# A two-block transformer kernel: two norms of the latent stream merged, and the matrix memory's unit loop reordered

## What is computed

```python
def rms_norm(x, gain=None):
    y = xf * lax.rsqrt(jnp.mean(xf * xf, axis=-1, keepdims=True) + EPS)
    ...
    y = y * gain
# end of block 1, start of block 2 (layer 0)
x = rms_norm(x, final_gain)
u_lat = rmsnorm(h_lat, norms[layer]) * (1 + scale_l[:, None]) + shift_l[:, None]
u_ctx = rmsnorm(h_ctx, norms[layer]) * (1 + scale_c) + shift_c
```

```python
w_intra = jnp.exp(logw - m_t[..., None])
qk = jnp.einsum('bhtd,bhsd->bhts', qc, kc) * w_intra
num = jnp.einsum('bhts,bhsv->bhtv', qk, vc) + ...
h = num / jnp.maximum(jnp.abs(den), jnp.exp(-m_t))[..., None]
```

## Time and profile before

| | us |
|---|---|
| median of 3 runs | 2748.92 (2747.24 to 2751.9) |
| the profiled execution, own time | 2751.43 |
| its span in the profile | 2749.6 |
| PE busy, share of the span | 91% |
| DVE busy | 60% |
| ACT busy | 37% |
| mean granted clock of PE | 0.969 |

### The profile page before, as it was taken

How to read it: one execution, slowest core, us unless ns; L and a number is a source line. 1 busy time by engine, 2 the same in 40 slices (tenths; PEclk the granted TensorE clock), 3 DMA queues, 4 the chain that set the end, 5 groups by cost and what they waited for, 6 DMA issues and landing times.

```text
span 2749.6 us, 49023 instructions
## 1 busy us (share of the span) xinstructions
PE 2509.0 (91%) x19510; PEld 2053.9 (75%) x19510; DVE 1650.3 (60%) x2694; ACT 1010.2 (37%) x1630; POOL 380.0 (14%) x336
## 2 busy tenths in 40 slices
PE   6999999978888799999899999889999998889976
PEld 4888877747777588888788887669987865667856
DVE  3777766465554577778677743665543335445665
ACT  4222223353342442222422223455444244334344
POOL 2000010114451200001100001020013500020041
PEclk8999999989999999999999999999999999989999
DMA  7666662200000256666466643225561320013401
GB/s 264 222 193 193 199 180 81 74 1 4 4 4 3 92 155 195 192 193 204 141 194 192 191 140 92 62 85 166 180 181 57 97 88 23 1 61 119 128 7 47
DMA packets 88429, 323.48 MB, mean 118 GB/s; under 512 B 9712, under 2 KB 10864, under 8 KB 87504
## 3 DMA queue, kind: packets, MB, share of 16 engines
q1 hardware_dynamic: 86864, 310.68, 36.5%
q0 software_dynamic: 1408, 10.59, 1.1%
HBM read 320.17 MB, written 1.05 MB: 117 GB/s over the span
## 4 chain that ended last, share of the span: by engine, by line
PE 82%; DVE 9%; ACT 5%; issue 2%; DMA 1%; DVEq 1%; POOL 0%; ACTq 0%; SPq 0%
PE bank L391 22%; PE bank L392 22%; PE bank L393 22%; PE bank L1770 3%; PE bank L1052 1%; PE bank L1043 1%; DVE row_statistics L1093 1%; DMA weight_ring<-stream_k 1%; PE bank L1066 1%; ACT work L1154 1%; ACT work L1163 1%; PE bank L1438 1%; PE bank L596 1%; DVE work L2655 1%; ACT weights_hi_lo L343 1%
## 5 line engine op out<-in xcount | busy, mean ns | idle before, releaser
L343 ACT ACTIVATE weights_hi_lo<-weight_ring 128x1024 fp32r<-128x1024 f32 (+1 forms) x388 | 404.0, 1042 | 1189.3 <-PE bank L393 1180.0
L391 PE MATMUL bank<-input_hi,weights_hi_lo 128*128 128x512 f32 (+1 forms) x2080 | 768.4, 369 | 44.6 <-DVE input_lo L622 38.7
L348 DVE TENSOR_TENSOR weights_hi_lo<-weight_ring,weights_hi_lo 128x1024 fp32r<-128x1024 f32 (+1 forms) x372 | 451.6, 1214 | 572.0 <-ACT weights_hi_lo L343 571.2
L392 PE MATMUL bank<-input_lo,weights_hi_lo 128*128 128x512 f32 (+1 forms) x2080 | 764.4, 368 | 0.0
L393 PE MATMUL bank<-input_hi,weights_hi_lo 128*128 128x512 f32 (+1 forms) x2080 | 763.7, 367 | 0.0
L391 PEld LDWEIGHTS bank<-input_hi,weights_hi_lo 128*128 128x128 f32 x2080 | 398.6, 192 | 117.5 <-issue 50.0
L392 PEld LDWEIGHTS bank<-input_lo,weights_hi_lo 128*128 128x128 f32 x2080 | 398.6, 192 | 62.5 <-issue 0.5
L393 PEld LDWEIGHTS bank<-input_hi,weights_hi_lo 128*128 128x128 f32 x2080 | 398.1, 191 | 62.9
L391 PE MATMUL bank<-hidden_hi_lo,weights_hi_lo 128*128 128x512 f32 (+1 forms) x960 | 345.4, 360 | 27.2 <-DVE hidden_hi_lo L832 17.6
L392 PE MATMUL bank<-hidden_hi_lo,weights_hi_lo 128*128 128x512 f32 (+1 forms) x960 | 343.9, 358 | 0.0
L393 PE MATMUL bank<-hidden_hi_lo,weights_hi_lo 128*128 128x512 f32 (+1 forms) x960 | 343.7, 358 | 0.0
(11 more groups left out here) (458 smaller groups left out, 2854.7 us busy)
## 6 DMA issues: line engine op xcount, KB each, us to landing
weight_ring<-stream_k SPq DMA_DIRECT2D x498, 512.0 KB, 3.5
weight_ring<-stream_f SPq DMA_DIRECT2D x64, 448.0 KB, 3.4
weight_ring<-stream_f SPq DMA_DIRECT2D x32, 512.0 KB, 3.7
extra_tiles<-condrows POOLq DMA_DIRECT2D x3, 1024.0 KB, 5.6
constants<-consts POOLq DMA_DIRECT2D x1, 2112.5 KB, 9.4
residual_stream<-xin SPq DMA_DIRECT2D x1, 2048.0 KB, 11.4
work<-nabias POOLq DMA_DIRECT2D x1, 2048.0 KB, 8.7
residual_stream<-ctx POOLq DMA_DIRECT2D x1, 1024.0 KB, 6.8
```

The source lines that it names most:

```text
L343: act.activation(split_place(place)[:, 0, 0:words], w[:, 0:words], ACT.Copy).then_inc(hi_ready, 1)
L348: eng.tensor_tensor(split_place(place)[:, 1, 0:words], ring[:, n % RING, 0:words], split_place(place)[:, 0, 0:words].bitcast(F32), ALU.sub ...
L391: pe.matmul(out, weights[:, 0, w], x_hi, start=first, stop=False)
L392: pe.matmul(out, weights[:, 0, w], x_lo, start=False, stop=False)
```

## The change

**Norms.** The gain norm and `norm 6` become one step, `two_norms_*`. While the feed-forward's last products run, ACT squares each tile twice: all 512 columns as it is, and the latent 256 columns with the gain on them (`gained_square`). POOL adds both kinds. PE sums both. The two roots are then made from one pair of sums: ACT takes the logarithm of the plain sum, DVE multiplies the square of the first root with the gained sum, ACT takes that logarithm, DVE adds the two, and ACT takes one exponential for all columns. The gain is folded into the modulation scale of the latent columns. The gained latent tiles themselves, which the residual stream needs later, are written by DVE after the norm (`gained_tiles_vector`, 8 instructions), ahead of the stage's loop. The second table load and the 8 squares behind the gain norm are gone.

**Matrix memory.** Rows and masked diagonals alternate between two places (`pb[0]` and `pb[5]`, two tiles `RD`), and there are three sets of weights. The scores of a head are made once for both directions (4 matmuls of 512, 512, 256 and 256 columns, in `pb[2]` to `pb[4]`) and no longer per unit. ACT waits for `sums(u-3)` where it waited for `normalise(u-2)`; PE's row waits for the exponentials of two units ago. DVE's loop now masks unit u+1 ahead of weighing unit u.

```diff
-                dve.wait_ge(qk_ready, u + 1)
+                dve.wait_ge(qk_ready, u // 2 + 1)
...
             for u in range(len(UNITS)):
-                weigh(u)
                 if u + 1 < len(UNITS):
                     mask_diagonal(u + 1)
+                weigh(u)
                 if u:
                     normalise(u - 1)
...
-                if u >= 2:
-                    act.wait_ge(unit_done, u - 1)
+                if u >= 3:
+                    act.wait_ge(sums_ready, u - 2)
...
-                if u:
-                    pe.wait_ge(exps_ready, u)
-                pe.matmul(pb[0][:, :], SELROW[:, 4 * d + h, :], RBR, start=True, stop=True).then_inc(rows_spread, 1)
+                if u >= 2:
+                    pe.wait_ge(exps_ready, u - 1)
+                pe.matmul(pb[ROW_BANKS[u % 2]][:, :], SELROW[:, 4 * d + h, :], RBR, start=True, stop=True).then_inc(rows_spread, 1)
...
             scores(0)
+            spread_rows(1)
             for u in range(len(UNITS)):
-                if u + 1 < len(UNITS):
+                if u and u + 1 < len(UNITS):
                     spread_rows(u + 1)
-                    scores(u + 1)
+                if u % 2 and u + 1 < len(UNITS):
+                    scores((u + 1) // 2)
                 sums(u)
```

```diff
+        def two_norms_scalar(act, x0):
...
+            act.wait_ge(summed, 7)
+            act.activation(logs, pb[2][:, :], ACT.Ln, bias=epsb[:, 0:1], scale=1.0 / D)
+            act.drain()
+            act.activation(squares, logs[:, a:b], ACT.Exp, scale=-1.0).then_inc(two_norms, 1)
+            act.activation(FIRST_RMS, logs[:, a:b], ACT.Exp, scale=-0.5)
+            act.wait_ge(two_norms_added, 1)
+            act.activation(squares, squares, ACT.Ln, bias=epsb[:, 0:1], scale=1.0 / D).then_inc(two_norms, 1)
+            act.wait_ge(two_norms_added, 2)
+            act.activation(pb[3][:, :], logs, ACT.Exp, scale=-0.5).then_inc(rooted, 1)
...
+        def two_norms_vector(dve):
...
+            dve.wait_ge(two_norms, 1)
+            dve.tensor_tensor(squares, squares, pb[0][:, 0:TC], ALU.mult).then_inc(two_norms_added, 1)
+            dve.wait_ge(two_norms, 2)
+            dve.tensor_tensor(logs, logs, squares, ALU.add).then_inc(two_norms_added, 1)
...
-            norm_scalar(act, 6, "l0_in", scaled, GAIN_NORMS[0][2] * KT + 1)
+            norm_scalar(act, 6, "l0_in", ffn_added, 4 + 3 * KT + 1)
```

More of the change, by code:

```diff
@@ L555, in norm_scalar @@
                 last_squares(act, cols, x_ready, x0, stage)
-            root(act, cols, bank, place)
+            if n != 6:
+                root(act, cols, bank, place)
             if n == 0:
@@ L574, in norm_scalar @@
                     ins.then_inc(modulated, 1)
-        ADDED_PLACES = [place for place in range(len(NORMS) + len(GAIN_NORMS)) if place != 7]
+        ADDED_PLACES = list(range(len(NORMS) + len(GAIN_NORMS)))
         def add_squares_gpsimd(pool, cols, place):
@@ new lines, in two_norms_tensor @@
+        def two_norms_tensor(pe):
+            pe.wait_ge(squares_added, ADDED_PLACES.index(6) + 1)
+            pe.matmul(pb[0][:, 0:TC], V("ones", 0, P), GAINED_SQ[:, 0, :], start=True, stop=False)
+            pe.wait_ge(gained_squared, KT)
+            pe.matmul(pb[0][:, 0:TC], V("ones", 0, P), GAINED_SQ[:, KT - 1, :], start=False, stop=True)
+            sum_squares(pe, ALL, 2, 6)
+        def two_norms_vector(dve):
+            a, b = LAT
+            logs, squares = WORK[:, 0, a:b], WORK[:, 1, 0:TC]
+            first_splits_vector(dve, "l0_in")
+            dve.wait_ge(two_norms, 1)
+            dve.tensor_tensor(squares, squares, pb[0][:, 0:TC], ALU.mult).then_inc(two_norms_added, 1)
+            dve.wait_ge(two_norms, 2)
+            dve.tensor_tensor(logs, logs, squares, ALU.add).then_inc(two_norms_added, 1)
@@ new lines, in gained_tiles_vector, with two_norms_gpsimd @@
+        def gained_tiles_vector(dve):
+            a, b = LAT
+            dve.drain()
+            for kt in range(KT):
+                dve.scalar_tensor_tensor(out=X[:, kt, a:b], in0=X[:, kt, a:b], scalar=V("fgain", kt), in1=FIRST_RMS,
+                                         op0=ALU.mult, op1=ALU.mult)
+        def two_norms_gpsimd(pool):
+            for kt in range(1, KT - 1):
+                pool.wait_ge(squared, 6 * KT + kt + 1)
+                pool.tensor_tensor(SQ[:, 0, :], SQ[:, 0, :], SQ[:, kt, :], ALU.add)
+                pool.wait_ge(gained_squared, kt + 1)
+                pool.tensor_tensor(GAINED_SQ[:, 0, :], GAINED_SQ[:, 0, :], GAINED_SQ[:, kt, :], ALU.add)
+                pool.drain()
+            pool.drain().then_inc(squares_added, 1)
@@ L1173, in build, with rotate @@
         q_copied, k_copied, v_copied = sem("mla_query_copied"), sem("mla_key_copied"), sem("mla_value_copied")
[L1174 to L1177 removed]
+        ODD_HEADS = 8
+        def rotate(dve, jobs, scale, scratch, turned, before=0):
             for i, (x, bank, cos, sin) in enumerate(jobs):
@@ L1182, in rotate @@
                                          op1=ALU.mult)
-                dve.wait_ge(turned, i + 1)
+                dve.wait_ge(turned, before + i + 1)
                 dve.scalar_tensor_tensor(out=tmp[:, TC:T], in0=bank[:, TC:T], scalar=scale, in1=sin, op0=ALU.mult,
@@ L2220, in mask_diagonal @@
                 dve.wait_ge(rows_spread, u + 1)
-                dve.tensor_tensor(tiles(RD), tiles(pb[0][:, :]), over(C("nu" if UNITS[u][0] == 0 else "nl"), TT), ALU.add)\
+                dve.tensor_tensor(tiles(RD[u % 2]), tiles(pb[ROW_BANKS[u % 2]][:, :]), over(C("nu" if UNITS[u][0] == 0 else "nl"), TT), ALU.add)\
                    .then_inc(rd_ready, 1)
```

105 lines of the change are left out of this document (64 added, 41 removed).

## The result

The changed kernel takes 2765.73 us (median of 5 runs, 2759.32 to 2770.22), beside 2750.94 for the kernel before on the same chip (5 runs, 2747.24 to 2752.16). The ratio is 1.0054, with a 95% interval of 1.0037 to 1.0071: slower by 14.8 us, between 10 and 20. The profiled execution has 2763.22 of its own, a span of 2761.4 and a mean granted clock of 0.965. That is 11.8 above the one before, where the sum said 11.1.

What follows compares the result with a forecast made beforehand. PE was 91% busy with 82% of the chain, but a short chain set the norms and a DVE-ACT circle the matrix memory. Norms -7.3 plus memory +18.4 (circle +6.4, clock +12) gave +11.1: 2760.0 us, range 2754 to 2768.

Steps and rivals of the forecast that it cites:

- Norms, -7.3: At the two norms: DVE's first scaling comes at 2061.26 instead of 2068.55, 7.3 us earlier.
- What this needs stays covered: Around the norms: doubled squares, POOL's doubled adds and DVE's gained tiles stay hidden, cost taken as zero.
- The later edges of the clock may differ by 1 us either way; zero taken: Behind the norms: later clock edges may shift time by 1 us either way, counted as zero.
- 1.6 us more of waiting: Before PE's products behind the norms: PE waits 4.3 us now and 1.6 more after, for four more steps.
- The circle at full clock, +6.4: Matrix memory: a pair takes 16.6 us instead of 12.72; +7.0, start +0.4, last sums -1.0, giving +6.4.
- The waits of 4.3 and 2.6: Matrix memory, each pair: PE waits 4.3 us before the even sums and 2.6 before the scores.
- The clock, +12: Matrix memory: PE's clock falls behind six waits, units 1 to 6, at 2.0 us each, +12.
- +3 and +26: Matrix memory's clock term: low end three falls at 1.0 us, high end six whole bursts at 1.2 GHz.
- The clock holds: Rival, matrix memory: full clock through most of the circle, one or two falls; +1, 2750 us; chance 0.18.
- The rows come in time: Rival, matrix memory: DVE's mask finds its row ready, a pair takes about 10.5 us; 2735 us; chance 0.10.
- The clock stays down: Rival, matrix memory: PE stays at 1.2 GHz for the stage; +25, 2774 us; chance 0.07.
- The norms give nothing back: Rival, norms: PE's products are held as long as before, +11 becomes +18; 2767 us; chance 0.05.

Runs made afterwards that it cites:

- memory only: The kernel before with only the matrix memory's new section, its two norms left as they were: 2772.12 us, ratio 1.0076.
- e8_adds_later: Changed kernel with row u+2 spread ahead of sums u, and POOL's gained adds of tiles 1 to 5 delayed to fall between DVE splits: 2737.64 us.
- e9_rows_old_norms: Kernel before with the new matrix memory, row u+2 spread ahead of sums u, and the old separate norms: 2743.75 us, ratio 0.9973.
- e4_rows_two_ahead: Changed kernel with PE spreading the row of unit u+2 ahead of the sums of unit u: 2734.18 us, ratio 0.9944 to the kernel before.
- e5_filled: Changed kernel with unread products filling PE's waits before even sums and odd scores, and ACT copying turned heads one unit earlier: 2751.63 us.
- e6_filled_long: Changed kernel with unread products filling only PE's long waits, before the sums of even units: 2759.49 us, ratio 1.0020 to the kernel before.
- e1_norms_only: Changed kernel with the old matrix memory, so only the two norms are merged: 2745.37 us, ratio 0.9982 to the kernel before.

## Why the prediction was right, and where it was not

**Norms, -7.3.** Measured -7.5 in their place: 15.29 to 7.78. From the last square to the scaling pass 6.82, for 7.04 in the sum. The step that failed is "What this needs stays covered", at zero. POOL's doubled adds were looked for between ACT and PE, where they cost nothing. They cost 0.9 by running into a split of DVE in the feed-forward before. The gained tiles are hidden: they end at 2075.86, and the next split starts at 2077.50. "The later edges of the clock may differ by 1 us either way; zero taken" came out at 0.5: PE waits 6.27 before its first product, where it waited 4.36, and over the first 5 us of products the granted clock is 0.50 (2062.5 to 2067.5), where it was 0.66 (2071 to 2076). From the first product to the copy of the values pass 280.77 us, for 280.30 before. (The prediction has 1.6 us more of waiting and so 5.9. Its own four added steps and their hand-overs make 1.9, which is what came.) So -7.5 + 0.9 + 0.5 = -6.1. The pairs of kernels that differ in the norms alone give, by their ratios, -4.9, -6.1 (changed, and memory only), -6.6 (`e8_adds_later` and `e9_rows_old_norms`) and -8.0 (`e4_rows_two_ahead` and `e9_rows_old_norms`). By their intervals the first is uncertain by about 2.4 us, the others by about 5, so they bear -6.1 out but can't tell it from -7.5.

**The circle at full clock, +6.4.** Measured +6.7 by `e5_filled`. There sums of odd units start 16.77 apart, for 16.6 in the sum, and from unit 1 to 7 pass 45.28 us (2357.11 to 2402.39), for 44.6. That makes +7.7 against the kernel before for +7.0, the start is +0.7 for +0.4, and the end -1.7 for -1.0. The waits of 4.3 and 2.6 are 4.23 and 2.44. The sum takes only one of the falls of the kernel before out, the last sums; what the longer circle costs with all of them out is the 10 us above.

**The clock, +12.** Measured +12.2 as the difference of two stages. Behind the six waits the bursts lost, against the same shapes at full clock, 2.6, 1.4, 0, 2.2, 1.5 and 2.2 (scores of 5.49, 2.85 and 4.39 for 2.85; sums of 3.87, 4.64 and 4.64 for 2.47). That is 9.9, or 1.65 for each where 2.0 was taken. The rest is one more fall, at the first sums behind a seventh wait of 2.44 (4.09 for 2.50, 1.6), which the sum had not counted, and what the bursts dragged along (a turned head 1.00 for 0.60, sums 2.75 for 2.40). By the section of the Trainium skill that the prediction names (page "TensorE: Matmul & The Clock Gate", section "HAM oscillation — how this bites in real kernels") every burst would start cold. The trace agrees for some and not for others (2.85 behind 2.44 us of waiting, 5.49 behind the same). So the total is hit within 0.2 by luck, by two errors that cancel: each fall too dear, and one fall missed. The ends that the prediction works out for this term, +3 and +26, would give 2751 and 2774; the stated range of 2754 to 2768 is a choice between them. Between two kernels with the same matrix memory, the changed one and the memory alone, the stage is the same to 0.1 (80.17, 80.24), and the same bursts run long (in the memory alone sums 3.95, scores 5.49, sums 3.84 and 4.64, scores 4.38, sums 4.64). So the pattern repeats between these two profiles; what decides which burst falls, no run here shows.

**Sum.** -6.1 + 6.7 + 12.2 = +12.8, for +11.8 between the profiled executions and +14.8 between medians. By place, the profiled executions differ by -1.2 up to the last split of the feed-forward (2053.26 and 2052.06), though 0.9 is lost there, by -7.5 in the norms, +0.5 up to the copy of the values, +18.9 in the stage and +1.1 behind it. So some 2 us of unexplained gain ahead of the norms and 1.1 of loss behind the stage lie between +12.8 and +11.8. Their cause stays open. The 3 us from there to the +14.8 of the medians lie within the interval. Of the 5.7 us between 2760.0 and 2765.73, 2.0 are the kernel before itself: 2748.92 in the three runs that the prediction had, 2750.94 in the five beside the changed kernel.

**The rivals.** *The clock holds* is refuted by a granted clock of 0.80 over the stage. *The rows come in time* is not what the changed kernel does, since each mask waits for its row. But `e4_rows_two_ahead` comes close to that case, built: 2734 for 2735, a pair 11.02 for 10.5. That the time fits is in part luck: three pairs save 5.1 us, not 6.6, but the whole stage is shorter by 10.0, of which about 2.9 are the falls of the clock in the kernel before. *The clock stays down* is refuted by the second scores at 1.00. *The norms give nothing back* is refuted by `e1_norms_only`.

## What to carry to other kernels

Buffering one thing twice helps only if each queue hands it out early: here both rows had a place, but PE issued the next one behind sums that waited for the weighing, and DVE's mask stood ahead of that weighing, so two in-order queues closed a circle. Moving the mask back took only the weighing out of it; moving the row ahead of the sums opened it. Before you move a waiting instruction forward, write down for one period who must be ahead of whom on every engine, and add up the ring. Where the ring leaves the matmul engine idle for some microseconds per period, count the clock too: it was about half of the loss here, and two thirds if the falls of the kernel before are not counted out.

## What was not expected of the hardware

- The same wait of PE gave different clocks: scores behind 2.53 us of idle took 5.46, 4.42 and 2.82 in one execution of `e6_filled_long`. In `e9_rows_old_norms` the sums of unit 6, behind 2.04 us of idle, took 4.11; in `e4_rows_two_ahead` they took 2.47 behind the same 2.04.
- Products that nobody reads made a kernel faster by 9 and 16 us.
- A POOL add of 0.74 us lengthened a DVE split beside it by 0.17, and each of five tiles of PE's products took 0.18 longer (8.25 for 8.07).
